# A late row transpose, an earlier activation and waits by quarters in the wide passes of a mixture-of-experts kernel

## The reference, cut to what matters

```python
def clamped_swiglu_expert(xb, w1, b1, w2, b2):
    h = xb @ w1 + b1
    x_glu = jnp.minimum(h[..., :D_FF], SWIGLU_LIMIT)
    x_lin = jnp.clip(h[..., D_FF:], -SWIGLU_LIMIT, SWIGLU_LIMIT)
    act = x_glu * jax.nn.sigmoid(SWIGLU_ALPHA * x_glu) * (x_lin + 1.0)
    return act @ w2 + b2
```

## Time and profile before

| | us |
|---|---|
| median of 3 runs | 2083.49 |
| lowest, highest | 2081.47, 2086.68 |
| the profiled execution, whole | 2084.6 |
| its span, first to last instruction | 2082.9 |

### The profile page before, as it was taken

The page is one execution under the profiler, slowest core; times in us unless marked ns, Lnnn a source line. Parts: engine busy times, 40 slices in busy tenths (PEclk is TensorE's granted clock), DMA queues, the critical chain, the costliest instruction groups (busy, mean ns, idle before and its releaser), DMA issues.

```text
span 2082.9 us, 35218 instructions
## 1 busy us (share of the span) xinstructions
PE 1971.4 (95%) x13189; PEld 1623.3 (78%) x13190; DVE 1000.4 (48%) x2418; ACT 451.0 (22%) x983; POOL 225.7 (11%) x220
## 2 busy tenths in 40 slices
PE   6999978977999999999999999999999999989996
PEld 3555533436778887788887888999999999979996
DVE  3998853344445554445454454444444434333332
ACT  3266654111111111111111111211111111110111
POOL 3111100001001010010100110110000100000000
PEclk9999979987999999999999999999999999999998
DMA  6000205235999999999999999998888878885651
GB/s 231 1 0 1 73 9 202 92 113 202 337 344 342 314 345 337 345 345 312 345 336 345 345 325 322 308 308 289 289 290 289 289 260 275 292 290 193 216 182 42
DMA packets 233940, 509.10 MB, mean 244 GB/s; under 512 B 7997, under 2 KB 12633, under 8 KB 233888
## 3 DMA queue, kind: packets, MB, share of 16 engines
q1 hardware_dynamic: 215264, 447.97, 60.1%
q0 software_dynamic: 16768, 59.98, 10.4%
q10 hardware_dynamic: 1856, 0.41, 0.1%
HBM read 475.53 MB, written 32.80 MB: 244 GB/s over the span
## 4 chain that ended last, share of the span: by engine, by line
PE 90%; DVE 4%; issue 2%; ACT 2%; DMA 1%; POOL 1%; SPq 0%; ACTq 0%; DVEq 0%; POOLq 0%
PE bank L1075 48%; PE bank L1115 12%; PE bank L1090 10%; PE bank L1304 5%; PE bank L1186 5%; DVE arena L835 2%; PE bank L1417 2%; PE bank L1222 2%; PE bank L1233 1%; PE bank L1103 1%; PE bank L1259 1%; PE bank L1408 1%; PE bank L1104 1%; DMA arena<-in_x 0%; PE bank L1280 0%
## 5 line engine op out<-in xcount | busy, mean ns | idle before, releaser
L1075 PE MATMUL bank<-arena 128*128 128x128 f32 (+5 forms) x8192 | 998.3, 284 | 20.8 <-issue 20.8
L1075 PEld LDWEIGHTS bank<-arena 128*128 128x128 f32 x8192 | 989.2, 192 | 33.4 <-issue 33.4
L734 DVE TENSOR_SCALAR arena<-bank,b1c 128x256 f32<-128x256 f32 x256 | 123.8, 483 | 478.1 <-PE bank L1075 478.1
L451 ACT ACTIVATE arena<-arena 128x256 f32<-128x256 f32 x256 | 106.6, 417 | 866.3 <-DVE arena L734 866.3
L1115 PE MATMUL bank<-arena 128*128 128x512 f32 x576 | 262.1, 593 | 0.0
L1090 PE MATMUL bank<-arena 128*128 128x144 f32 (+4 forms) x1792 | 252.0, 294 | 4.6 <-DVE arena L746 4.4
L1047 DVE TENSOR_SCALAR arena<-bank,cols 128x256 f32<-128x256 f32 x256 | 112.1, 479 | 283.4 <-PE bank L1417 283.4
L1090 PEld LDWEIGHTS bank<-arena 128*128 128x128 f32 x1792 | 237.1, 190 | 7.8 <-DVE arena L746 7.7
L342 POOL DMA_INDIRECT out<-arena,idx_cur x64 | 99.0, 1548 | 873.1 <-DVE arena L778 863.3
L835 DVE SCALAR_TENSOR_TENSOR arena<-arena,cols 128x512 f32<-128x512 f32 (+1 forms) x226 | 182.3, 807 | 16.5 <-ACT arena L544 9.5
L1115 PEld LDWEIGHTS bank<-arena 128*128 128x128 f32 x576 | 102.5, 190 | 94.7 <-issue 90.4
(11 more groups left out here) (218 smaller groups left out, 1114.5 us busy)
## 6 DMA issues: line engine op xcount, KB each, us to landing
arena<-in_w SPq DMA_DIRECT2D x192, 2048.0 KB, 11.4
arena<-in_b SPq DMA_DIRECT2D x32, 512.0 KB, 11.0
arena<-in_x SPq DMA_DIRECT2D x16, 512.0 KB, 7.3
token_rows<-arena SPq DMA_DIRECT2D x8, 528.0 KB, 2.9
out<-arena SPq DMA_DIRECT2D x8, 512.0 KB, 5.8
arena<-in_w_in SPq DMA_DIRECT2D x2, 1536.0 KB, 13.3
arena<-in_w_in SPq DMA_DIRECT2D x1, 3072.0 KB, 19.7
arena<-in_w_out SPq DMA_DIRECT2D x1, 2048.0 KB, 8.3
```

Source lines behind the costliest of these rows:

```text
L451: a.activation(sg[:, m % 2, :], g1[:, m % 2, :], ACT.Sigmoid, scale=ALPHA).then_inc(sg_ready, 1)
L734: v.tensor_scalar(g1[:, r, :], bank[r][:, 0:SLOTS], b1c[:, m:m + 1], LIMIT, ALU.add, ALU.min).then_inc(g1_ready, 1)
L1075: last = mm(bank[m % 2][:, side * SLOTS:side * SLOTS + n], w1_sb[:, k, lo:lo + P], xT[:, k, 0:n], start=k == 0, stop=k == KD - 1)
```

## The change

Three edits. On VectorE, `hidden_b(6)` goes ahead of `hidden_a(7)`, in all passes. On TensorE, in wide passes, `trans_y(4)` and `trans_x(3)`, which stood between blocks 6 and 7, go behind block 7: `trans_y(4)` to `trans_y(7)`, then `trans_x(3)` as the pass's last work. And in all passes the one wait for all of `xT` at the head becomes four, each ahead of the first matmul that reads a quarter.

```diff
@@ dve_pass @@
             for m in range(1, MT):
                 hidden_a(m)
-                hidden_b(m - 1)
+                if m < MT - 1:
+                    hidden_b(m - 1)
+                if m == MT - 2:
+                    hidden_b(m)
@@ pe_pass @@
-            pe.wait_ge(xt_ev, q4)
             for m in range(MT):
...
                 for side in range(2):
                     lo = side * FF + m * P
                     for k in range(KD):
+                        if m == 0 and side == 0 and k % 2 == 0:
+                            pe.wait_ge(xt_ev, q4 - 3 + k // 2)
                         last = mm(bank[m % 2][:, side * SLOTS:side * SLOTS + n],
...
             down(6, range(MT))
-            trans_y(4)
+            down(7, range(MT))
+            for d in range(4, KD):
+                trans_y(d)
             trans_x(q4, 3)
-            down(7, range(MT))
-            trans_y(5)
-            trans_y(6)
-            trans_y(7)
```

## The result

The changed kernel takes 2067.65 us (median of 4 runs, 2066.02 to 2069.51) beside 2085.09 us for the kernel before (4 runs, 2081.47 to 2089.25): a ratio of 0.9919, with a 95% interval of 0.9905 to 0.9933. That is 17 us less, within 14 and 20. The forecast was 2071.2 us and 12.3 us less, the range 2065.5 to 2077.0; it started from 2083.49 us, the median of three of these four runs of the kernel before. By the two profiled executions the gain is 15.1 us (span 2082.9 and 2067.8, whole times 2084.6 and 2069.51).

A forecast was written before the change was run, and what follows sets the result against it. TensorE, busy 95% of the span, was taken as the bound. Activation 8.7 plus pass end 4.3 minus 0.7 at the kernel's end gives 12.3 us: 2071.2 us against the median of 2083.49, range 2065.5 to 2077.0.

The forecast's parts named there:

- The activation: Activation 6 ahead of tile 7's eviction removes TensorE's wait as wide passes' down part begins, no new wait: 8.7 us.
- The pass end: Transposes moved behind block 7 in wide passes: 0.33 us gained at each of thirteen boundaries, 4.3 us, between 2.9 and 8.5.
- the term of issue: At a wide pass's end, the sequencer issues four transposes at 0.06 us each plus one register step: 0.33 us.
- issue costs nothing: Bound at the wide pass boundary: TensorE's own work sets the next start, R + 0.66, R being when `trans_y(7)` may start; 0.65 us gained.
- The last quarter: Wait at the first tile's 13th record: `xT` whole 0.5 us earlier, so cost 0, at worst 0.1 in three passes.
- The end of the kernel: Last pass: `trans_y(7)` may start 0.66 us earlier but `y_ready` comes 1.35 later behind it, nothing hides it: -0.7 us.
- either way: One low-clock spell more or less among the tier changes is ordinary: 1.7 us in either direction.
- The one of the clock at the boundaries: Rival: transposes in a row and the hole behind lower the clock at thirteen boundaries, 22 us lost, 2093; chance 0.02.
- The one of the tier change: Rival: code moves, another tier change meets the long branch, 2081.8 us (chance 0.04), or this one goes, 2060.6 (0.03).
- The one in which everything is hidden: Rival: the loop end at wide pass boundaries hides all four transposes, 8.5 us gained there, 2067.0 us; chance 0.10.
- Did nothing: Case that the edits do nothing: 2083 us; chance 0.02.
- the last quarter waits: Rival: VectorE's late eviction makes each boundary lose 0.9 us, 11.7 back, 2082.9 us, no change; chance 0.05.

The follow-up runs named there:

- second pair of traces: The changed kernel and the kernel before, each run once more unchanged for a second trace: 2068.32 us and, in one execution, 2082.41 us.

## Why the prediction was right, and where its sizes were off

**The activation.** Right in mechanism and size: 8.7 us forecast, 8.3 by the steps of the traces; the 9.0 of the pass lengths has clock in it. No wait took its place, as worked out from the 29th record.

**The pass end.** The mechanism was right, the term of issue was too dear. 0.33 us were put down for four transposes and a register step; measured are 0.80 - 0.65 = 0.15. The step taken as the nearest row, 0.06 us between the two weight loads of `trans_y(7)`, is not what the sequencer needs for an issue: its records put the register step behind `trans_y(7)` at 1583.43 and the one behind four more transposes at 1583.54, so the four were issued in 0.11 us. A boundary gave 0.51 in place of 0.33, thirteen of them 6.7 in place of 4.3. The bound "issue costs nothing", 0.65 a boundary, was nearer than the value taken; 0.14 us of loop end stay bare, and the version with `trans_y(7)` last takes 0.12 us off a pass of n = 144.

**The last quarter.** Right: no hole at the 13th record. The eviction was ready 0.5 us before, as worked out; the experiment with one wait shows what it would cost, 1.22 us at nine boundaries.

**The end of the kernel.** -0.7 forecast. The span from `trans_y(7)` to the end of the bias grew from 3.2 to 4.4 us, that is 1.2 with 0.66 won ahead of it: -0.6. Behind the scatter this pair of traces then differs by 0.8 the other way (11.91 and 11.14 us), which is scatter by the second trace of the kernel before (11.02).

**What the sum left out.** With its terms as measured the passes and the end should have given 8.3 + 6.7 - 0.6 = 14.4; the traces differ by 18.1 from the first pass on. 1.7 are the spell of clock at the start of tier 152, which the prediction held to be ordinary scatter "either way" and which went with the old pass end. Nor is it why the profiled execution took 1.1 us more than the median: the second trace of the kernel before, 2082.41 us long, has the spell as well. 1.2 lie in pass 29, behind the empty tier: the clock was granted at 0.51 for the first 5.8 us behind its first load before (1871.2 to 1877.0), and for 3.2 us after (1859.5 to 1862.7). In the second pair of traces the two passes 29 differ by 0.4 us in this, so much of it is chance. 0.8 are the last landing at the end, and 0.1 the narrow passes. The first pass started 3.0 us later in this trace, which brings the 18.1 down to 15.1.

So some 3 us of the gain are clock that the prediction didn't forecast, and that is luck. The time would have lain in its range without them too.

**The rivals.** The one of the clock at the boundaries was wrong in sign: the change removed a spell. The one of the tier change didn't come about: 9.77 us ahead of tier 176 in place of 9.68. The one in which everything is hidden (2067.0) was close in time to the measured 2067.65, but not for its reason: 6.7 of its 8.5 us came from the boundaries, and the clock gave the rest. "Did nothing" and "the last quarter waits" are excluded by the traces.

## What to carry to other kernels

Read the holes of the bounding engine by releaser and give each one work of its own: here a reordering filled the wait for another engine, and two groups of transposes filled a wait and a loop end. Work that covers a sequencer's loop end should stand ahead of the last instruction that waits: here the sequencer went on when that wait was met, 0.35 us before the engine got there. And work that is moved to the end of a pass needs its consumer's wait split, or it comes back as a wait at the head of the next.

## What the runs showed of the hardware that was not expected

- Four transposes, eight instructions, were issued in 0.11 us, while TensorE took 0.44 us to run them.
- A branch over the code of one unused tier cost 8 us of hole, and 1.5 us more in the pass behind it, whose clock was partly at its lower level: 9.65 us in all.
- With a hole of 0.28 us ahead of one of 2.03 to 2.08 us the granted clock fell behind it in five of five traces. With a first hole of under 0.1 us it fell in none of nine, of which one has a second hole as long.
